# Second attention: V products in steps of two key blocks, PSUM banks given out by use

## The reference

```python
# MLA: 8 heads, query and key of 96, value of 64
sc = einsum('bqhd,bkhd->bhqk', qblk, k) * scale      # causal, -1e30 above the diagonal
p = softmax(sc); o = einsum('bhqk,bkhd->bqhd', p, v)
# differential: 4 heads, two maps each, query and key of 32, value of 64
p = softmax(sc)                                       # per map, causal
a = p[:, :, 0] - lam * p[:, :, 1]
o = einsum('bhqk,bkhd->bqhd', a, v); o = rms_norm(o, subln_g) * (1.0 - lam_init)
# memory: 4 heads of 64 over 256 memory tokens, not causal
p = softmax(sc); o = einsum('bhsm,bmhd->bshd', p, v)
y = concatenate([y_mla, y_diff, y_mem]) * silu(z);  x = x + y @ w_out
```

## Time and profile before

| | us |
|---|---|
| median of 3 runs | 3510.32 |
| lowest and highest | 3502.98 and 3512.49 |
| the profiled execution | 3510.73 |
| its span | 3509.0 |
| second attention in it | 3050.8 to about 3404 |
| of that MLA, differential, memory | 146.7, 157.5, 49.0 |
| output product behind it | 3404 to 3509 |

### The profile page before, as it was taken

The page is one execution under the profiler, slowest core; times in us unless marked ns, Lnnn a source line. Parts: engine busy times, 40 slices in busy tenths (PEclk is TensorE's granted clock), DMA queues, the critical chain, the costliest instruction groups (busy, mean ns, idle before and its releaser), DMA issues.

```text
span 3509.0 us, 36793 instructions
## 1 busy us (share of the span) xinstructions
PE 3242.2 (92%) x14026; PEld 2462.4 (70%) x14026; DVE 1841.2 (52%) x3008; ACT 969.7 (28%) x1810; POOL 900.7 (26%) x566
## 2 busy tenths in 40 slices
PE   7999999877789998989999999998998999799988
PEld 3577788555557886668887788887867887465457
DVE  1499993467664447871331544444233416766661
ACT  2320111366651003560101100001213212655450
POOL 0133233000002324653332433332233342200002
PEclk9999999999999999999999999999999899898799
DMA  8012233100001111112332111112111110000011
GB/s 211 13 45 66 90 99 96 72 18 7 19 19 49 50 35 43 37 54 97 98 136 87 41 49 48 48 48 102 60 55 62 60 48 27 1 1 13 0 58 75
DMA packets 185861, 196.37 MB, mean 56 GB/s; under 512 B 12257, under 2 KB 152029, under 8 KB 184029
## 3 DMA queue, kind: packets, MB, share of 16 engines
q1 hardware_dynamic: 170669, 142.08, 13.7%
q10 hardware_dynamic: 15024, 51.98, 4.0%
HBM read 153.15 MB, written 40.89 MB: 55 GB/s over the span
## 4 chain that ended last, share of the span: by engine, by line
PE 68%; DVE 10%; issue 9%; POOL 4%; ACT 4%; DMA 2%; DVEq 2%; ACTq 1%; POOLq 1%; SPq 0%
PE psum L629 65%; DVE arena L1689 3%; PE psum L633 3%; DVE rounded L1689 2%; DVE arena L1692 2%; DVE arena L1846 2%; POOL stat L1174 1%; POOL arena L1228 1%; ACT arena L1300 1%; DMA arena<-z_d 1%; POOL rounded L1185 1%; DVE arena L1834 1%; POOL arena L1245 1%; ACTq L1306 0%; DVEq L1842 0%
## 5 line engine op out<-in xcount | busy, mean ns | idle before, releaser
L629 PE MATMUL psum<-rounded,rounded 128*128 128x512 f32 (+2 forms) x9504 | 2214.7, 393 | 106.4 <-DVE rounded L1689 84.8
L629 PEld LDWEIGHTS psum<-rounded,rounded 128*128 128x128 f32 x9504 | 1799.5, 190 | 514.0 <-issue 95.9
L629 PE MATMUL psum<-arena 128*128 128x512 f32 (+15 forms) x2450 | 779.0, 487 | 56.8 <-ACT arena L1300 40.7
L1183 POOL CAST rounded<-arena 128x1024 fp32r<-128x1024 f32 (+1 forms) x190 | 206.4, 1087 | 1717.8 <-DMA arena<-in_w_in 815.4
L629 PEld LDWEIGHTS psum<-arena 128*128 128x128 f32 (+4 forms) x2450 | 399.7, 202 | 321.0 <-issue 277.8
L1300 ACT ACTIVATE arena<-psum 128x512 f32<-128x512 f32 (+9 forms) x572 | 310.1, 568 | 863.0 <-PE psum L629 711.8
L1185 POOL TENSOR_TENSOR rounded<-arena,rounded 128x1024 fp32r<-128x1024 f32 (+1 forms) x190 | 465.3, 2449 | 28.2 <-issue 1.3
L633 PE MATMUL psum<-ident,arena 128*128 128x128 f32 (+1 forms) x1816 | 284.7, 301 | 86.6 <-DVE arena L1689 30.3
L633 PEld LDWEIGHTS psum<-ident,arena 128*128 128x128 f32 (+1 forms) x1816 | 234.1, 154 | 156.9 <-issue 51.6
L1689 DVE TENSOR_TENSOR arena<-arena,psum 128x512 f32<-128x512 f32 (+1 forms) x176 | 125.8, 733 | 354.9 <-PE psum L629 335.3
L1689 DVE TENSOR_TENSOR rounded<-arena,rounded 128x1024 fp32r<-128x1024 f32 (+1 forms) x132 | 198.6, 1536 | 210.0 <-ACT rounded L1303 209.4
(11 more groups left out here) (137 smaller groups left out, 1487.4 us busy)
## 6 DMA issues: line engine op xcount, KB each, us to landing
arena<-in_w_in SPq DMA_DIRECT2D x84, 512.0 KB, 3.7
arena<-in_w_ffn_up SPq DMA_DIRECT2D x44, 512.0 KB, 3.8
arena<-in_w_ffn_down SPq DMA_DIRECT2D x22, 512.0 KB, 3.6
z_d<-arena ACTq DMA_DIRECT2D x32, 256.0 KB, 3.0
gate_d<-arena ACTq DMA_DIRECT2D x16, 512.0 KB, 3.8
arena<-in_w_ssm_out SPq DMA_DIRECT2D x16, 512.0 KB, 4.2
arena<-z_d SPq DMA_DIRECT2D x8, 1024.0 KB, 4.8
arena<-gate_d ACTq DMA_DIRECT2D x16, 512.0 KB, 3.5
```

What stands on the lines that cost most here:

```text
L629: return pe.matmul(out, lhsT, rhs, start=start, stop=stop)
L1183: pool.tensor_copy(high_part, raw)
```

## The change

The V products of the second attention are cut into pieces of two key blocks, one piece a step, as the first attention has them. `PV_LAG` goes from 7 to 6. A sweep of eight key blocks takes four steps from `n + 6` on; a sweep of four takes two steps, from `n + 7` on (`late`); memory has two key blocks and one step, `n + 6`. The last differential sweep keeps its eight blocks in one step. All products of a sweep add up in the same bank, and only the last piece tells VectorE. `pair_end` and `STEPS2` follow from the new table. The banks are divided: four for scores, three for transposes (and for the pair's small sums), one for outputs. ScalarE's and VectorE's code is the same; the step of the output read follows `summed_at`.

```diff
--- before.py
+++ after.py
@@ -585,7 +585,7 @@
         blocks2 = [n for n, u in enumerate(subs2) if not first_map(u)]
         subs4 = [n for n, u in enumerate(subs2) if u["ph"] == "e"]
         sweeps2 = [n for n in blocks2 if subs2[n]["i"] % 4 == 3]
-        T_LAG, PV_LAG = 5, 7
+        T_LAG, PV_LAG = 5, 6
 
         sweeps1 = [n for n, u in enumerate(units1) if u["i"] % 4 == 3]
         T_LAG1, PV_LAG1 = 4, 5
@@ -610,9 +610,16 @@
             return sweep_of(subs2[done[-1]]) if done else None
 
         turned_at = {n + T_LAG: n for n in blocks2}
-        summed_at = {n + PV_LAG: n for n in sweeps2}
-        STEPS2 = len(subs2) + PV_LAG + 2
-        pair_end = {j: max(n for n in sweeps2 if subs2[n]["ph"] == "d" and subs2[n]["h"] == 2 * j + 1) + PV_LAG + 1
+        last_diff = max(n for n in sweeps2 if subs2[n]["ph"] == "d")
+        summing_at = {}
+        for n in sweeps2:
+            keys, late = (2, 0) if subs2[n]["ph"] == "e" else (subs2[n]["nk"], subs2[n]["nk"] == 4)
+            each = keys if n == last_diff else 2
+            for m in range(keys // each):
+                summing_at[n + PV_LAG + late + m] = (n, m * each, m * each + each, keys)
+        summed_at = {s: n for s, (n, _, end, keys) in summing_at.items() if end == keys}
+        STEPS2 = max(summed_at) + 3
+        pair_end = {j: 1 + max(s for s, n in summed_at.items() if subs2[n]["ph"] == "d" and subs2[n]["h"] == 2 * j + 1)
                     for j in range(2)}
 
         def last_group(u):
@@ -1042,7 +1049,7 @@
             for s in range(STEPS2):
                 if s < len(subs2):
                     u, name = subs2[s], ("S", N1 + s)
-                    out = bank(name, 1 if u["nk"] <= 4 else 2)
+                    out = bank(name, 1 if u["nk"] <= 4 else 2, FOR_SCORES)
                     pe.wait_ge(*vacated(name))
                     pe.wait_ge(*vacated(name, -1))
                     if u["ph"] == "e":
@@ -1059,24 +1066,26 @@
                     pe.wait_ge(probs_ready, N1 + blocks2.index(n) + 1)
                     for grp in range(last_group(u) + 1):
                         spots = [2 * m + grp for m in range(4)] if u["ph"] == "e" else range(4 * grp, min(4 * grp + 4, u["nk"]))
-                        four(("T", N1 + n, grp), [probs[:, b * P:(b + 1) * P] for b in spots])
-                if s in summed_at:
-                    n = summed_at[s]
+                        four(("T", N1 + n, grp), [probs[:, b * P:(b + 1) * P] for b in spots], FOR_TURNED)
+                if s in summing_at:
+                    n, b0, b1, keys = summing_at[s]
                     u, name = subs2[n], sweep_of(subs2[n])
                     first = 4 * (u["i"] // 4)
                     pT = pT2[u["i"] // 4]
-                    pe.wait_ge(*written(("T", N1 + n, last_group(u))))
-                    out = bank(name)
-                    pe.wait_ge(*vacated(name))
-                    keys = 2 if u["ph"] == "e" else u["nk"]
-                    for b in range(keys):
+                    if b0 == 0:
+                        pe.wait_ge(*written(("T", N1 + n, last_group(u))))
+                        bank(name, 1, FOR_SUMS)
+                        pe.wait_ge(*vacated(name))
+                    out = psum_of(name)
+                    for b in range(b0, b1):
                         lo = max(0, b - first) * P if u["ph"] != "e" else 0
                         last = mm(out[:, lo:512], u["v"](b), pT[:, b, lo:512], b == 0, b == keys - 1)
-                    last.then_inc(full(name), 1)
+                    if s in summed_at:
+                        last.then_inc(full(name), 1)
                 for j in range(2):
                     if s == pair_end[j] + 2:
                         pe.wait_ge(sub_squared, j + 1)
-                        out = bank(("ss", j))
+                        out = bank(("ss", j), 1, FOR_TURNED)
                         pe.wait_ge(*vacated(("ss", j)))
                         for tt in range(TT):
                             last = mm(out[:, 2 * tt:2 * tt + 2], odsq[:, j, tt * P:(tt + 1) * P], head_pair)
@@ -1084,7 +1093,7 @@
                     if s == pair_end[j] + 8:
                         pe.wait_ge(sub_spread, j + 1)
                         for half in range(2):
-                            four(("sr", j, half), [rs_wide[:, j, 4 * half + n, :] for n in range(4)])
+                            four(("sr", j, half), [rs_wide[:, j, 4 * half + n, :] for n in range(4)], FOR_TURNED)
             end_phase(pe)
             pe.wait_ge(phase_done, 4 * 10)
             for c in range(2):
```

## The result

The changed kernel takes 3532.02 us, the median of six runs (3530.08 to 3539.6), where the kernel before took 3510.23 beside it (3502.98 to 3514.24, six runs): a ratio of 1.0067, with a 95% interval of 1.0053 to 1.0081. It is slower by some 22 to 24 us, where 3494.5 was forecast, and outside the range. The profiled execution of the changed kernel took 3539.6 us, its slowest; 5.5 us of its distance lie ahead of the attention, in code that both kernels share, so the three parts are compared by themselves. (The prediction called more than 2 us there a sign of something missed. It is none: in the fifteen profiled executions of this document the attention begins anywhere from 3043.7 to 3058.3 us, behind the same code.)

A forecast was written before the change was run, and what follows sets the result against it. TensorE was taken to bound MLA; in the differential part TensorE and VectorE wait in turn, with clock falls and V bursts costing time. 0 - 11.2 + 4.0 - 2.6 - 4.0 - 2.4 = -16.2, from 3510.7 to 3494.5 us, range 3486 to 3503.

The forecast's parts named there:

- The sweep-of-eight term: Differential part: spreading the sweep over four steps hides 2.8 us of VectorE work, four times: -11.2 us.
- The first rival: Differential part: TensorE keeps the pace and nothing is gained; 3509.7 us, chance 0.24.
- The banks, taken as 0: MLA: three transpose banks could cost 0.7 us a head, +5.6, but moved V pieces hide it; four score banks also 0.
- The first piece: Differential sweep of eight: ScalarE's copy just fits behind one score tile, so the new wait is 0, at most 0.2 us.
- The overlap, +4.0: Differential part: V pieces part three score-tile pairs a head that overlapped; 1.0 us a head, +4.0 us.
- the estimate made from it, +7.0: Differential part: loss from parted pairs counted at full overlap, 4 x 1.76 = +7.0 us in place of +4.0.
- The sweep of four, -2.6: Differential part: its last 384 columns fill TensorE's hole before the transposes; -0.66 us, four times, -2.6 us.
- the clock, -4: Differential part: a shorter hole may prevent some clock falls; a third of 12 us, -4 us.
- the cold sum: Differential part: time at half clock, 75 us before, should be 60 to 75 us.
- Memory, -2.4: Memory part: the last differential sweep starts a step sooner, halving ScalarE's 6.0 us wait; -2.4 us.
- The slower rival: Differential part: pieces too short to raise the clock; +13.8 us, 3524.5 us, chance 0.12.
- 98 were to decide: Differential part: cold stretches of about 98 us instead of 75 would show the pieces too short to raise the clock.

The follow-up runs named there:

- the version that keeps the pairs: The changed kernel with the differential sweep of eight in two pieces of four blocks at n + 7 and n + 9, sweep of four whole: 3528.65 us, ratio 1.0062.
- the evenly spread form: The changed kernel with differential pieces of two key blocks only at every second step, behind the transposes: 3497.18 us, ratio 0.9973 to the kernel before.

## Why the prediction was wrong, point by point

**The sweep-of-eight term, -11.2.** This is the step that failed first. It said "What follows is limited by VectorE as long as the clock is up" and counted 2.8 us of VectorE work a sweep as won. TensorE was idle for only 7.8 us of the differential part, and the prediction had that row before it. Hiding VectorE's work can give back no more than TensorE's idle time, unless TensorE's own work gets shorter. Nor were the waits all of 6.0 us: the six measure 1.5, 6.0, 1.7, 4.4, 4.7 and 0.6. Two of the long ones, in the third and the fourth head:

```profile
3289.92 0.69 DVE L2237 COPY arena<-psum 64x512 f32<-64x512 f32 x1 [4.38 <-PE psum L629]
3333.96 0.68 DVE L2237 COPY arena<-psum 64x512 f32<-64x512 f32 x1 [4.68 <-PE psum L629]
```

Against whole sweeps with the same banks the pieces made the differential part 7.0 us longer, where -11.2 + 4.0 - 2.6 - 4.0 = -13.8 was forecast for it. The waits for the output went as forecast, and came back as waits for score tiles, 14.9 to 54.6 us. The first rival, that TensorE keeps the pace, described this, but at 3509.7 us.

**The banks, taken as 0.** This is the larger miss. By themselves they cost 31 us, and with the MLA pieces in place 19.1 of the 23.2 us that the three parts of the change lose. (No run has the pieces with all eight banks shared, so their share is known for whole sweeps alone.) For MLA the cover (V pieces of the sweep before) was right and the price nearly so, +5.6 against +7.0: 155.1 us without pieces, 147.9 with them, and one wait left in the first head. For the rest the prediction looked for waits, found VectorE not full and wrote 0. The direct waits are indeed small (5.3 us for VectorE's reads). What it left out is the clock: 122.3 us cold with whole sweeps and divided banks instead of 82.8.

**The first piece, "at most 0.2".** ScalarE's copy was to fit behind one score tile. In the second head the piece waited 1.02 us for it, because the second group of transposes had itself waited 0.56 us for a bank; over the part TensorE waited 2.7 us in such places.

**The overlap, +4.0.** The mechanism was right and its size too small. Against the version that keeps the pairs the change loses 9.8 us at equal cold time, 8.2 of it busy time, where the bound was 7.0 for all four heads. The bound took full clock; some of the pairs run at half clock, which would make them dearer. The kernel before with eight pairs parted, 6.4 us more busy time, gives the same order of size. By the Trainium skill, "TensorE: Matmul & The Clock Gate", Part 3 on packing small matmuls, products on different row groups run at once; the estimate made from it, +7.0, was nearer than +4.0. The twelve matmuls that took 3.38 us with the pair together and 4.53 us with it parted agree with its direction; the second time is longer than lost overlap alone explains.

**The sweep of four, -2.6, and the clock, -4.** Neither came: the cold sum was 78.5 us instead of 60 to 75. More V products at the hole did not keep the clock up in this form; the evenly spread form did, with 37.5 us.

**Memory, -2.4.** It became 7.1 us longer; half of the 13.4 us more at half clock is 6.7. ScalarE's wait of 6.03 us was not halved. It no longer ends with the V products themselves but with the transposes that come behind them and a score tile:

```profile
3406.78 1.08 ACT L1309 ACTIVATE arena<-psum 128x512 f32<-128x512 f32 x2 [6.75 <-PE psum L640]
```

**The slower rival.** The side came true by luck, the mechanism did not: short pieces did not keep the clock from rising (78.5 us cold, where 98 were to decide), and with whole sweeps and the same banks it was cold for longer, 88.7 us. The change is slower by 23.2 us in the three parts for two other reasons: 8.2 us are half of the 16.3 us more at half clock, and 15.0 us are the last column of the table. Whole sweeps with the same banks have nothing of these 15.0, so they come with the differential pieces: busy time as of parted pairs, and waits that the rings make only together with the pieces.

**The sum itself.** It was made against the profile and ends at 3494.5; the 0.4 us that the prediction said it must take off to stand at the median were left on. That changes nothing here.

What stays open: why dividing the banks lengthens the cold stretches when TensorE's idle time in the differential part doesn't change (7.8 and 7.9 us). The same page of the Trainium skill has, in its section "A second HAM failure mode: psum-queue depth-cycling", a kernel whose clock swings because of small idle times around its banks; here the swing grew without more idle time, so no run shows that this is the cause.

## What to carry to other kernels

Before work is counted as won because another engine will do it meanwhile, compare the gain with the idle time of the engine that stays busy: it can't exceed that unless the clock changes or that engine's own work gets shorter. In a part that runs partly at half clock, do the sum twice: once for work and waits, once for half of the cold time; here the second made the evenly spread version faster, and most of the loss of every regrouping of banks with whole sweeps. Where a long burst of dense products can be cut up, spread it evenly over the sparse stretches, and put each piece where it separates nothing that runs side by side.

## What the runs showed of the hardware

**Time at half clock cost up to half of its length.** The last column of the table shows it for the sum of the three parts: the kernel before, the whole sweeps with divided banks and the evenly spread version differ by up to 33 us in length, and by 0.7 us once half of the cold time is taken off. The Trainium skill, "TensorE: Matmul & The Clock Gate", Part 1, gives the same price for throttled time; these three sums agree with it. The other kernels say less, since their order of work or their added products change the rest (the whole column goes from 313.5 to 335.5), and single parts agree less closely. The memory part took 57.1 us with 2.0 us cold before, and 69.4 and 72.1 us with 34.0 and 33.4 us cold in the two kernels where it was cold longest, so 0.39 and 0.48 us for each us at half clock.

**The order of small work moves the clock.** With the same matmuls, the cold time of the differential part went from 37.5 us (pieces behind transposes at every second step) to 102.4 us (pieces between score tiles at every second step), although TensorE was idle for 7.1 us in the first and 0.9 us in the second. In the spread version six more products of 512 columns kept the memory part at full clock up to its last 3.8 us.

**A part can be slow because of what ran before it.** With the same banks, the same memory steps and the same last sweep, the memory part took 64.2 us behind the differential pieces of the change and 67.3 us behind whole sweeps; it was at half clock for 15.4 and 28.7 us.
